# A two-layer hybrid trunk in one program: taps transformed by one stacked product, bias as a row of the inverse, and new orders at four joints

## What is computed

```python
def conformer_conv(x, w_in, b_in, dw, dw_b, ln_g, ln_b, w_out, b_out):
    h = x @ w_in + b_in                      # 2048 -> 4096
    a, gate = jnp.split(h, 2, axis=-1)
    h = a * jax.nn.sigmoid(gate)
    h = causal_dwconv(h, dw, dw_b)           # 31 taps per feature, bias dw_b
    h = jax.nn.silu(layer_norm(h, ln_g, ln_b))
    return h @ w_out + b_out
# diff_attention: qkv, partial rotary, softmax(1) - lambda softmax(2), times v,
#                 RMSNorm per head, @ w_o
# conv_ffn: (silu(causal_dwconv(x @ w_gate)) * (x @ w_up)) @ w_down
# each is x = x + part(rms_norm(x)), and out = rms_norm(x)
```

## Time and profile before

| quantity | value |
|---|---|
| median of 3 runs | 2175.75 us (2175.35 to 2176.8) |
| the profiled execution's own time | 2175.13 us |
| its span | 2173.3 us |
| mean granted PE clock, share of full speed | 0.996 |
| PE busy | 2144.0 us, 99% of the span |
| DVE, ACT busy | 1449.7 us, 1044.7 us |
| DMA traffic | 399.57 MB, mean 184 GB/s |

### The profile page before, as it was taken

How to read it: one execution, slowest core, us unless ns; L and a number is a source line. 1 busy time by engine, 2 the same in 40 slices (tenths; PEclk the granted TensorE clock), 3 DMA queues, 4 the chain that set the end, 5 groups by cost and what they waited for, 6 DMA issues and landing times.

```text
span 2173.3 us, 30564 instructions
## 1 busy us (share of the span) xinstructions
PE 2144.0 (99%) x11078; PEld 1822.1 (84%) x11078; DVE 1449.7 (67%) x2131; ACT 1044.7 (48%) x1479; POOL 40.1 (2%) x50
## 2 busy tenths in 40 slices
PE   8999999999999999999999999999999999999998
PEld 7788788888888888888888877888888888888886
DVE  5556767777777774544688866667777777764543
ACT  6444555544454444444554443554544454444443
POOL 7000000000000000000000000000000000000000
PEclk9999999999999999999999999999999999999999
DMA  7555356666666665555655544466666666656553
GB/s 246 196 188 189 129 181 177 191 193 185 185 190 193 184 187 199 184 192 189 187 168 174 185 162 155 155 188 183 190 192 184 185 192 193 183 194 217 189 190 110
DMA packets 513852, 399.57 MB, mean 184 GB/s; under 512 B 6535, under 2 KB 425313, under 8 KB 513505
## 3 DMA queue, kind: packets, MB, share of 16 engines
q1 hardware_dynamic: 513600, 398.67, 59.1%
q10 hardware_dynamic: 192, 0.07, 0.0%
HBM read 396.61 MB, written 2.10 MB: 183 GB/s over the span
## 4 chain that ended last, share of the span: by engine, by line
PE 96%; DVE 1%; DMA 1%; SPq 1%; ACT 1%; issue 0%; DVEq 0%; ACTq 0%
PE acc L1352 35%; PE acc L1357 17%; PE acc L1383 12%; PE acc L1384 12%; PE acc L1385 12%; PE acc L1610 1%; PE acc L1612 1%; PE acc L1611 1%; DMA sb_stage<-in_conv_w_in 1%; PE aux L1399 0%; PE aux L1621 0%; PE aux L1448 0%; PE aux L1569 0%; ACT sb_w_hi L519 0%; DVE sb_w_lo L820 0%; PE aux L1466 0%
## 5 line engine op out<-in xcount | busy, mean ns | idle before, releaser
L820 DVE TENSOR_TENSOR sb_w_lo<-sb_stage,sb_w_hi 128x1024 fp32r<-128x1024 f32 x744 | 907.2, 1222 | 532.8 <-ACT sb_w_hi L519 529.2
L519 ACT ACTIVATE sb_w_hi<-sb_stage 128x1024 fp32r<-128x1024 f32 x744 | 781.8, 1053 | 679.4 <-PE acc L1385 392.7
L1352 PE MATMUL acc<-sb_normed,sb_w_hi 128*128 128x512 f32 x3264 | 1027.4, 396 | 0.0
L1357 PEld LDWEIGHTS acc<-sb_normed,sb_w_lo 128*128 128x128 f32 x3264 | 613.1, 188 | 144.9
L1357 PE MATMUL acc<-sb_normed,sb_w_lo 128*128 128x256 f32 x3264 | 641.4, 278 | 0.0
L1352 PEld LDWEIGHTS acc<-sb_normed,sb_w_hi 128*128 128x128 f32 x3264 | 497.7, 189 | 0.6
L1383 PE MATMUL acc<-sb_w_hi,sb_hidden 128*128 128x512 f32 x688 | 267.9, 389 | 0.0
L1385 PE MATMUL acc<-sb_w_hi,sb_hidden 128*128 128x512 f32 x688 | 267.7, 389 | 0.0
L1384 PE MATMUL acc<-sb_w_lo,sb_hidden 128*128 128x512 f32 x688 | 267.7, 389 | 0.0
L525 ACT ACTIVATE sb_corr<-acc 128x256 f32<-128x256 f32 x204 | 76.9, 377 | 210.5 <-PE acc L1357 210.4
L1385 PEld LDWEIGHTS acc<-sb_w_hi,sb_hidden 128*128 128x128 f32 x688 | 129.1, 188 | 27.0
(11 more groups left out here) (185 smaller groups left out, 1612.7 us busy)
## 6 DMA issues: line engine op xcount, KB each, us to landing
sb_stage<-in_ffn_w_gate SPq DMA_DIRECT2D x86, 1024.0 KB, 5.4
sb_stage<-in_ffn_w_up SPq DMA_DIRECT2D x86, 1024.0 KB, 5.4
sb_stage<-in_ffn_w_down SPq DMA_DIRECT2D x80, 1024.0 KB, 4.9
sb_stage<-in_attn_w_qkv SPq DMA_DIRECT2D x48, 1024.0 KB, 5.3
sb_stage<-in_conv_w_in SPq DMA_DIRECT2D x31, 1024.0 KB, 6.4
sb_stage<-in_conv_w_out SPq DMA_DIRECT2D x16, 1024.0 KB, 4.9
sb_stage<-in_attn_w_o SPq DMA_DIRECT2D x16, 1024.0 KB, 4.9
sb_stage<-in_ffn_w_down SPq DMA_DIRECT2D x8, 768.0 KB, 4.3
```

The lines of the kernel that those rows point to most:

```text
L519: nc.scalar.activation(w_hi[:, (2 * first + h) % PIECES, 0:size], stage[:, first % STAGES, off:off + size], ACT.Copy).then_inc(hi_ready, 1)
L820: nc.vector.tensor_tensor(w_lo[:, slot, 0:size], stage[:, first % STAGES, off:off + size], w_hi[:, slot, 0:size].bitcast(F32), ALU.subtrac ...
L1352: nc.tensor.matmul(acc[:, bank, :], w_hi[:, slot, q * P:(q + 1) * P], operand[:, k, :], start=begin, stop=False, skip_group_check=True)
L1357: return nc.tensor.matmul(acc[:, bank, T:2 * T], w_lo[:, slot, q * P:(q + 1) * P], operand[:, k, 0:T], start=False, stop=end, skip_group_c ...
```

## The change

- **Taps.** The taps are loaded three times, at partitions 0, 32 and 64 of a 96-row tile that DVE clears first, and the tap matrix is repeated three times in `dft_in`. ACT rounds both to float32r (`taps_hi`), DVE replaces one third of each by its low part (`taps_lo`), and one product over 96 rows gives high*high + high*low + low*high. The eight products move to steps 5 to 8, the parameters to step 9.
- **Start.** Block 4 is loaded ahead of `dft_in` and the taps; x is turned and split earlier, the squares of x move to steps 2 and 3, and the first `keep_clock` goes from 18 to 10.
- **Bias.** The convolution bias enters as one more row of the inverse (a row of ones in the matrix, a row of `prod` loaded by SP, cleared by POOL); ACT copies the result out of PSUM and DVE only measures.
- **Joint to `conv_out`.** ACT keeps the chunks, DVE measures the last one from PSUM, the split of block 1 is ordered anew, and the clock products are 10 + 4 + 4.
- **Value stage.** `keep_v` goes ahead of the split, both `outputs` and both `o_stats` come together, ACT takes both `heads_hi` in step 2, DVE both `heads_lo` between the halves of step 3; the wait for the last probabilities moves to the first `outputs`; `wo` starts on the heads of turns 0 and 1.
- **End.** The last block of `down1` is multiplied for token block 0 first, then for block 1 (`last_block`), and statistics, scaling and stores follow per token block.

```diff
@@ transform_rows
-        out[0:taps, 6 + h, 0:m] = kernel[part, taps - 1 - np.arange(taps)].T
+        for copy in range(3):
+            out[32 * copy:32 * copy + taps, 6 + h, 0:m] = kernel[part, taps - 1 - np.arange(taps)].T
+    out[m, 2, :] = 1.0
@@ SP
-            sp.dma_start(rows_t[:, :], conv_dw[0]).then_inc(taps_loaded, 16)
+            conv_in_block(STAGES)
             sp.dma_start(dft_in[:, :, :], dft_rows).then_inc(dft_loaded, 16)
+            sp.wait_ge(rows_cleared, 1)
+            for n in range(3):
+                sp.dma_start(rows_t[32 * n:32 * n + TAPS, :], conv_dw[0]).then_inc(taps_loaded, 16)
             load_in_rows(0)
-            for at in range(STAGES, 2 * STAGES):
+            for at in range(STAGES + 1, 2 * STAGES):
                 conv_in_block(at)
             load_in_rows(1)
+            load_dw_bias(0)
...
-            for scaled_rows, cols in ((tail_scaled, slice(D - WIDE, D)), (row_scaled, slice(0, D - WIDE))):
-                for b in range(TB):
+            for b, scaled_rows, cols in ((0, tail_scaled, slice(D - WIDE, D)), (0, row_scaled, slice(0, D - WIDE)),
+                                         (1, row_scaled, slice(0, D - WIDE)), (1, tail_scaled, slice(D - WIDE, D))):
@@ ACT
+            def keep_conv(c, b, banks):
+                act.wait_ge(inverse_done, TB * c + b + 1)
+                if (c, b) == (CH - 1, TB - 1):
+                    act.wait_ge(conv_measured, TB * CH)
+                nc.scalar.activation(conv[:, b, WIDE * c:WIDE * (c + 1)], banks[:, b, :], ACT.Copy).then_inc(conv_kept, 1)
+            def taps_hi():
+                act.wait_ge(taps_loaded, 16 * 3)
+                act.wait_ge(dft_loaded, 16)
+                nc.scalar.activation(kern_op[:, :, :], dft_in[0:STACK, 6:8, :], ACT.Copy).then_inc(taps_high, 1)
+                nc.scalar.activation(taps_op[:, :], rows_t[:, :], ACT.Copy).then_inc(taps_high, 1)
...
                 hi(0, (0, at + 2), 0)
-                if at < 2:
-                    x_hi(at + 2)
-                if at < X_PARTS:
-                    x_squares(at)
+                if at in (2, 3):
+                    x_squares(2 * (at - 2))
+                    x_squares(2 * (at - 2) + 1)
                 if at == X_PARTS:
+                    taps_hi()
                     rms_root(STAT["input"])
...
                 hi(0, (0, at + 2), 1)
+                if at < 2:
+                    x_hi(at + 2)
...
             glu_hi(last)
+            for b in range(TB):
+                keep_conv(last - 1, b, acc)
             prod_hi(last, 0)
             prod_hi(last, 1)
             hi(0, (0, B["conv_out"] + 1), 0)
             warm_up(ACT.Sqrt)
-            hi(0, (0, B["conv_out"] + 1), 1)
+            keep_conv(last, 0, aux)
...
+            keep_conv(last, 1, aux)
             warm_up(ACT.Silu, 1)
+            hi(0, (0, B["conv_out"] + 1), 1)
@@ ACT, v_turn
                     elif j == 0 and not first:
                         squares_of(i - 1, 0)
+                        squares_of(i - 1, 1)
                     elif j == 1 and not first:
                         root_of(i - 1, 0)
-                        squares_of(i - 1, 1)
+                        root_of(i - 1, 1)
                     elif j == 2 and not first:
-                        root_of(i - 1, 1)
                         heads_hi(i - 1, 0)
-                    elif j == 3 and not first:
                         heads_hi(i - 1, 1)
@@ DVE
+            def taps_lo():
+                dve.wait_ge(taps_high, 2)
+                nc.vector.tensor_tensor(kern_op[64:STACK, :, :], dft_in[64:STACK, 6:8, :],
+                                        kern_op[64:STACK, :, :].bitcast(F32), ALU.subtract).then_inc(taps_ready, 1)
+                nc.vector.tensor_tensor(taps_op[32:64, :], rows_t[32:64, :], taps_op[32:64, :].bitcast(F32),
+                                        ALU.subtract).then_inc(taps_ready, 1)
...
                 lo(0, (0, at + 2), 0)
...
+                if at == X_PARTS:
                     row_squares(STAT["input"])
-                if at == X_PARTS:
+                    taps_lo()
                     row_scales(STAT["input"], True)
...
                 if q == 1:
                     for k in range(2):
                         norm_split(k)
+                    lo(0, (0, B["conv_out"] + 1), 0)
+                if q == 2:
+                    for k in range(2, 4):
+                        norm_split(k)
                     lo(0, (0, B["conv_out"] + 1), 1)
@@ DVE, v_turn
-                    lo(0, (0, B["v"] + 4 * i + j + 2), 0)
                     if j == 0 and not first:
                         keep_v(i - 1)
+                    lo(0, (0, B["v"] + 4 * i + j + 2), 0)
+                    if j == 3 and not first:
+                        heads_lo(i - 1, 0)
+                        heads_lo(i - 1, 1)
                     lo(0, (0, B["v"] + 4 * i + j + 2), 1)
@@ PE
-                    pe.wait_ge(taps_loaded, 16)
-                    pe.wait_ge(dft_loaded, 16)
+                    pe.wait_ge(taps_ready, 2)
...
-                nc.tensor.matmul(aux[0:HALF, n % BANKS, :], dft_in[0:TAPS, 6 + n % 2, 0:HALF],
-                                 rows_t[:, WIDE * (n // 2):WIDE * (n // 2 + 1)], start=True, stop=True
+                nc.tensor.matmul(aux[0:HALF, n % BANKS, :], kern_op[:, n % 2, 0:HALF],
+                                 taps_op[:, WIDE * (n // 2):WIDE * (n // 2 + 1)], start=True, stop=True
...
-                if 4 <= at < 8:
-                    halfway = lambda: (turn_taps(2 * (at - 4)), turn_taps(2 * (at - 4) + 1))
-                elif at == 8:
+                if 5 <= at < 9:
+                    halfway = lambda: (turn_taps(2 * (at - 5)), turn_taps(2 * (at - 5) + 1))
+                elif at == 9:
                     halfway = turn_params
...
-            keep_clock(aux[:, 3, 0:P], 16)
+            keep_clock(aux[:, 3, 0:P], 10)
+            for b in range(TB):
+                pe.wait_ge(ln_ready, b + 1)
+                keep_clock(aux[:, 3, 0:P], 4)
...
-            pe.wait_ge(prob_kept, HEADS)
...
-            project("wo", heads_op, KD, [(0, OPER["wo"] - 4), (KD - 4, OPER["wo"] - 2), (KD - 2, OPER["wo"])], last_heads)
+            project("wo", heads_op, KD, [(0, OPER["wo"] - 8), (KD - 8, OPER["wo"] - 4), (KD - 4, OPER["wo"] - 2),
+                                           (KD - 2, OPER["wo"])], last_heads)
```

More of the change, by code:

```diff
@@ L609, in _ @@
                     open_gate(c)
-                if 4 <= at < 8:
-                    keep_taps(2 * (at - 4))
-                    keep_taps(2 * (at - 4) + 1)
+                if 5 <= at < 9:
+                    keep_taps(2 * (at - 5))
+                    keep_taps(2 * (at - 5) + 1)
+                if 0 < c < CH - 1 and j == 6:
+                    for b in range(TB):
+                        keep_conv(c - 1, b, aux)
                 if at == 7:
@@ L1002, in _ @@
             for b in range(TB):
-                keep_conv(last - 1, b, acc)
-            lo(0, (0, B["conv_out"] + 1), 0)
+                measure_conv(last - 1, b)
             for b in range(TB):
-                keep_conv(last, b, aux)
-                own.wait()
+                measure_conv(last, b)
+                dve.wait_ge(conv_measured, TB * last + b + 1)
                 nc.vector.bn_aggr(ln_mean[:, b, :], ln_sum[:, b, :, :]).then_inc(ln_ready, 1)
@@ L1080, in project @@
                         norm_low(name, before, gain)
-                    if at in ends:
+                    if at in ends and (gain is not None or ends[at] < CH - 1):
                         evict(name, ends[at], at)
@@ L1280, in v_turn @@
                         o_sums(i - 1, 0)
+                        o_sums(i - 1, 1)
                     elif j == 1:
                         o_scale(i - 1, 0)
-                        o_sums(i - 1, 1)
                     elif j == 2 and not first:
                         o_scale(i - 1, 1)
-                    elif j == 3 and not first:
-                        heads_lo(i - 1, 0)
-                        heads_lo(i - 1, 1)
             own.turn(0, MAXIMA + COMBINE)
@@ L1387, in wide_block, with last_block @@
                     ins.then_inc(pieces_done, 1)
+            def last_block(name, operand, tiles):
+                at = CH * NB[name] - 1
+                n, first = B[name] + at, C[name] + TB * (CH - 1)
+                pe.wait_ge(lo_ready, 2 * n + 2)
+                for b in range(TB):
+                    bank = (first + b) % BANKS
+                    for k in range(tiles - depth(n), tiles):
+                        h, q = divmod(k - KB * ORDER[name][at][1], KB // 2)
+                        slot, wide = (2 * n + h) % PIECES, slice(WIDE * q, WIDE * (q + 1))
+                        high, low = operand[:, k, b * P:(b + 1) * P], operand[:, k, T + b * P:T + (b + 1) * P]
+                        nc.tensor.matmul(acc[:, bank, :], high, w_hi[:, slot, wide], start=False, stop=False)
```

(20 more changed lines are left out.)

142 lines of the change are left out of this document (97 added, 45 removed).

## The result

| | kernel before | changed kernel |
|---|---|---|
| median of the runs compared | 2176.22 us (2175.17 to 2177.39) | 2185.65 us (2184.02 to 2186.33) |
| ratio, 95% interval | | 1.0043 [1.0032, 1.0053] |
| span of the profiled execution | 2173.3 us | 2183.3 us |
| mean granted PE clock | 0.996 | 0.991 |

The changed kernel is 0.43% slower. The forecast's sum was 2187.6 us, its range 2179 to 2195.

A forecast was written before the change was run, and what follows sets the result against it. PE, busy 99% of the span, was taken to bound the kernel. From the profiled execution, 2175.1 + 20.3 - 2.4 - 2.6 - 0.8 - 2.0 = 2187.6 us; the likeliest case ranges from 2179 to 2195.

The forecast's parts named there:

- input stage: Start of the kernel: three tap loads of 11.7 us on one DMA engine hold block 5 until 63.7; +20.3 us.
- joint to `conv_out`: Joint before `conv_out`: shorter DVE chain, third tile earlier by 2.7 us, or 1.7 if the clock falls; taken as -2.4 us.
- value stage: Attention values: probabilities wait gone, first `keep_v` early, 1.2 us stalls of turns 1 and 2 stay; -2.6 us.
- `wo`: Products of `wo`: first no longer waits, `outputs` does; -1.8 us at most, about 0 if the clock drops; taken as -0.8.
- end: Last block and stores: token block 0 done earlier, less left to store behind block 1; -2.0 us (0 to -3).
- the copies are cheaper than the first: Rival on the input stage: tap loads cost 9.9 us each, total 2182 us; no chance of its own given.
- my 0.83 case: Likeliest case, chance 0.83: slower by the queue, in its sizes, ending between 2179 and 2195 us.
- the prediction's first two terms: Value stage: -1.7 us from the vanished wait for probabilities, -1.2 us from `keep_v` of turn 0 coming early.
- Side by side: Rival on the start: the three tap loads run on different engines, input stage -4.1 us, total 2163.2 us; chance 0.13.
- The queue holds SP: Rival on the start: blocks 5 to 7 issued late, up to +6 us, total 2193; no chance of its own given.
- the window of one engine: Sign in the input stage: a window of 25 us with DMA share 0.07 and 22 GB/s would show the forecast right.
- an odd row count: Reason given for the tap loads: a load with an odd number of rows runs on one DMA engine, always the same.

The follow-up runs named there:

- experiment 3: Kernel before with its one tap load made three, the two others read by nothing: 2196.18 us, ratio 1.0094.
- experiment 2: Changed kernel with one tap load instead of three, low-order tap terms left out: 2166.25 us, ratio 0.9952.
- experiment 7: Changed kernel with each tap load as 16 and 15 rows, and DVE's second-head `o_scale` moved from turn step 2 to 1: 2151.07 us, ratio 0.9886.
- experiment 6, first part: Changed kernel with its three unsplit tap loads issued from GpSimd's software queue instead of SP's: 2159.57 us, ratio 0.9921.
- experiment 5: Changed kernel with each tap load as 21 and 10 rows, single execution: 2160.14 us.

## Why the prediction was right

Shifts are the changed kernel's time at a point less that of the kernel before at the same one.

| step | predicted | measured | read at |
|---|---|---|---|
| input stage, to the inverse of the last chunk | +20.3 | +17.1 | 236.34 against 219.26 |
| joint to `conv_out`, third tile | -2.4 | -1.8 | 259.97 against 244.72: +15.3 |
| value stage, first `outputs` | -2.6 | -3.3 | 1287.26 against 1275.28: +12.0 |
| `wo` | -0.8 | 0.0 | last `o_stats`, 1374.65 against 1362.66: +12.0 |
| end | -2.0 | -2.0 | span, +10.0 |

**The start.** The mechanism stood as predicted: one engine, block 5 held, PE idle for some 20 us and again for 4, a window with share 0.06 or 0.07. The size of one term was off. I took 11.7 us per tap load from the 13.0 us between two landings, less 1.3 for `dft_in`, and charged it three times. A further load costs 9.3 us (experiment 3) or 9.5 (experiment 2). In the changed kernel `dft_in` lands at 24.9 and block 5 at 58.8; less 1.3 for `in_rows` and 2.6 for the block, the three take 30.0 us, 10 each. The rival "the copies are cheaper than the first", which I priced at 9.9 us and 2182, was nearest, with the lower edge of my 0.83 case. The full-block rate of 25 KB per us was the better row, because it holds nothing but transfer; the gap between two landings also holds some 2 us that come once, and no run here shows what they are. Block 5 came 4.9 us before its predicted 63.7, the chain behind it took 11.8 us as against 11.7, so PE's product behind the first tap pair came 4.8 us before its forecast. From there to the middle of block 8 it took 19.7 us, where the sum had 18.0 and 1.0 for the lower clock: the clock cost 1.7. So the middle of block 8 was 16.2 late and not 20.3. Another 0.9 us was lost up to the inverse; 0.6 of it is a new wait for the parameters, whose `keep` had moved on by one block:

```profile
102.60 0.46 PE L1584 MATMUL aux<-sb_glu_op,sb_dft_hi 128*118 128x512 f32 x1 [0.61 <-DVE sb_par_f L1049]
```

**The joint to `conv_out`.** PE's timeline answers the earlier trace rows:

```profile
255.59 0.77 PE L1483 MATMUL acc<-sb_w_hi,sb_conv_op 128*128 128x512 f32 x1 [2.14 <-DVE sb_conv_op L1011]
...
259.97 0.39 PE L1483 MATMUL acc<-sb_w_hi,sb_conv_op 128*128 128x512 f32 x1
```

The first product is 2.0 us earlier in the frame of this joint, where I had 1.7. Of the two values that I gave for the third tile, -2.7 and -1.7, the second came: the twelve products took 4.4 us again, at the lower clock, and I had leaned to the first.

**Value stage and `wo`.** Turns 1 and 2 gained nothing, by the chain through `heads_hi` that I had worked out: periods of 26.66 and 26.75 us against 26.69 and 26.68, and experiment 7 shows that it is this chain. Of the -3.3 at the first `outputs`, 0.2 lie ahead of the stage (its first product is at 1258.32 against 1243.25, +15.1). The other 3.1 stand against 2.9 from the prediction's first two terms; the 0.15 that moving `o_stats` was to give back per turn does not show. The wait moved from `wo`'s first product to `outputs`:

```profile
1367.55 0.67 PE L1744 MATMUL aux<-sb_probs_t,sb_v_tok 128*128 128x256 f32 x2 [3.99 <-DVE sb_v_tok L1322]
```

At 1367.55 the changed kernel is 10.3 us late, 1.7 ahead of its shift before, the -1.8 of the prediction; the lower clock behind the wait gives all of it back, the other of the two ends that I had named. The -0.8 lay between the two ends, and one of them came.

**The end** came out as worked: 9.05 us from the last product to the end where it was 11.04.

**The rivals.** "Side by side" (2163, chance 0.13) did not happen on the queue that the change uses. On another kind of queue (experiment 6, first part) the time comes near it, but there each load is spread, and not each on an engine of its own. "The queue holds SP" is true of SP, which issued block 5 near 31.2 us, but it added nothing, since the landing came 27.4 us behind that and the chain behind the landing had its predicted length. One sum among the rivals was off: by the prediction's own terms the second and third load would cancel the rest of the change at 5.5 to 6 us each, not 4.5. Nothing turned on it, as they cost 9.3 to 10. And of the signs that I named, the window of one engine was broken by bursts and ran at 25 GB/s, not 22: the 22 were read from the 43-row loads of `rows_f`. The prediction's reason, an odd row count, is wrong (experiment 5), though for 31 rows it gives the same one engine.

## What to carry to other kernels

Before a load is duplicated or moved in a queue, look at the DMA share while it runs: a share near 1/16 for microseconds means one engine. Everything behind it on the queue that has a part on this engine waits, and a load on another hardware queue only gets packets in between: beside large packets it is hardly sooner. Choose row counts that spread (16 and 15 in place of 31), or issue the load from the software queue. And where an engine takes work earlier in its order, move the producer of that work too: one call moved in DVE's order was worth 8.2 us, more than twice what the whole regrouping gained in the value stage.

## What was not expected of the hardware

- The same 31-row loads run on one engine from the queues of SyncE (share 0.06, 25 GB/s) and ScalarE (0.06, 25 GB/s), and spread from GpSimd's (66.7% of the 16 engines from 24 to 26 us, 7.3 us to landing, block 5 not held).
- Spread over all engines, the tap loads still move only 134 to 155 GB/s at a share of 0.96 to 1.09, against 410 GB/s for the weight blocks in the same trace. All of them read the same 248 KB; whether that is the reason was not tried.
- A block on another hardware queue than the slow loads landed as late as behind them on the same queue: block 5 at 57.9 us against 58.8. The engine took the packets of the two queues in equal number (10 and 10 from 50 to 54 us), so the queue with 8 KB packets moved four times the bytes of the one with 2 KB packets.
